# A two-block transformer kernel: modulation rows, attention values and latent key products placed in column groups of the array

## The chip, the cores and the metric

One core of one Trainium2 chip runs the whole program; the other cores are idle. The metric is the device time of one execution in microseconds (us). Three runs of the kernel before took 3384.53, 3387.52 and 3387.95 us; the median is 3387.52 us.

## What is computed

The input is 512 tokens of width 1024. A first block of two layers (latent attention next to a causal convolution, cross attention over 256 memory tokens, a gated FFN) is followed by a second block of one layer (modulated delta-rule mixer, 16 experts with expert choice). The change touches only what stands in the first half of each layer of the first block:

```python
kv = (rms_norm(c_kv, kv_norm_g) @ w_ukv).reshape(B, S, MLA_HEADS, QK_NOPE_DIM + V_HEAD_DIM)
k_nope, v = kv[..., :QK_NOPE_DIM], kv[..., QK_NOPE_DIM:]      # 8 heads, 64 + 64
...
s = q_nope @ k_nope + q_rope @ k_rope                          # per head, chunk-causal
p = softmax(mask(s * scale));  o = p @ v                       # query blocks of 128
...
def adaln_params(cond, w_mod, b_mod):                          # second block, for c and for c_ctx
    return jnp.split(jax.nn.silu(cond) @ w_mod + b_mod, 6, axis=-1)
```

The modulation rows `silu(cond) @ w_mod` (two condition vectors, 1024 x 6144 weights) belong to the second block but are computed during the attention of the first one, half of them in each layer.

## The kernel before

All operands of the products named here are f32. Each engine has its own instruction list, and semaphores (`Signal`, with `at(layer, n)` the n-th event of this layer) order them. PSUM has eight banks `ps[0..7]` of 128 partitions x 512 columns. An engine's list is worked through strictly in order, so an instruction that waits holds back all that stands behind it. The two layers of the first block are one `Fori` loop; what is said of one holds for both.

**Latent products** (PE, from L850 on). With 8 heads: for each head a query product into `ps[h]` (96 rows out, two contraction tiles), then for each head a key product into `ps[h][0:64]` (64 columns of weights, two contraction tiles `k`), then for each of four token tiles a value product into `ps[t]`. ACT copies each result out (L1478, L1481, L1484). Then PE multiplies every query head by a swap matrix (L878), DVE multiplies by the sine (L2049), POOL multiplies by the cosine and adds (L1828, L1831): the rotary embedding. Only when all eight heads are rotated does ACT begin with the exponentials.

**Attention loop.** Step n = 4 x head + query tile, n = 0 to 31. On DVE, each step is: `maximum(n)` (mask L2059, row maximum L2061, scaling L2063), `reciprocal(n-1)` (L2069, which waits for the exponential of step n-1), `tap(n)` (four of the 31 x 4 multiply-adds of the convolution, L2076/L2080), and, at steps 11, 15, 19, ..., `head_out(n//4 - 2)` (L2086), which copies the finished head out of `ps[4][0:64]` and raises `pv_ev`. The last two heads are copied after step 31. On ACT, `exps(h)` is four exponentials (L1496) with the normalisation of older steps between them (L1506); then follow the copy of a modulation row out of PSUM (L1527) and `turned_probs(h-1)`, four copies of transposed probabilities (L1514); then `exps(h+1)`. The order on ACT thus is: exps(h+1), modulation row h, turned probabilities of head h, exps(h+2). On PE the loop is

```python
scores(0); scores(1)
for h in range(HEADS):
    if h < MOD_CHUNKS: modulation_rows(h)      # MOD_CHUNKS = 6
    if h + 2 < HEADS:  scores(h + 2)
    values(h)
    if h < MOD_CHUNKS: modulation_turn(h)
```

`modulation_rows(i)` is eight products (L922) of 2 weight columns by 512 columns into `ps[4][64:66]`; from i = 1 on it waits for `mod_row_ev`, ACT's copy of the row before. `scores` (L893) waits for exponentials to free its banks. `values(h)` transposes the probabilities (L904), four sets of 4, 3, 2, 1 blocks, waits for `pv_ev` of the head before, and multiplies by the values (L911): four products of 512, 384, 256 and 128 columns into `ps[4][0:64]`. `modulation_turn` (L931) turns a row of 512 into four columns with 2 x 128 weights.

After the loop PE computes the keys and values of the cross attention (L766), and then the residual products.

**Traces.** One f32 product shows as two MATMUL and two LDWEIGHTS (PEld) records, so the eight products of `modulation_rows` are sixteen records, the four of `values` are eight.

Of the kernel before, what the change touches and what calls it, by code (L numbers as in the profile page):

```python
# [24 lines left out]
ACT = mybir.ActivationFunctionType  # L25
# [3 lines left out]
P = 128  # L29
D = 1024  # L30
KT = D // P
S = 512
# [63 lines left out]

K_ID, K_ONE, K_SWAP = 0, P, 2 * P
K_FREQ = 3 * P
N_FIRST = K_FREQ + 1
K_TRI, K_STRICT = N_FIRST, N_FIRST + 2 * P  # L100
K_SAME = K_STRICT + 2 * P
K_HALF = K_SAME + P
# [6 lines left out]
def shape_constants():  # L109
    c = np.zeros((P, NCONST), np.float32)  # L110
    i = np.arange(P)
    same = (i[:, None] // CHUNK) == (i[None, :] // CHUNK)
    c[:, K_ID:K_ID + P] = np.eye(P)
    c[:, K_ONE:K_ONE + P] = 1.0
    h = ROPE // 2
    for j in range(h):
        c[NOPE + h + j, K_SWAP + NOPE + j] = -1.0
        c[NOPE + j, K_SWAP + NOPE + h + j] = 1.0
    before = i[:, None] <= i[None, :]
    for d, m in enumerate((before, before.T)):  # L120
        c[:, K_TRI + d * P:K_TRI + (d + 1) * P] = m & same
        c[:, K_STRICT + d * P:K_STRICT + (d + 1) * P] = m & same & (i[:, None] != i[None, :])
    c[:, K_SAME:K_SAME + P] = same

    for u in range(2 * DH):
        for n in range(2):
            c[:, K_HALF + 2 * u + n] = (i // CHUNK) == (n if u < DH else 1 - n)
    c[:, K_IOTA:K_IOTA + CAP] = np.arange(CAP) + 1
    freq = np.float32(10000.0) ** (-np.arange(0, ROPE, 2, dtype=np.float32) / np.float32(ROPE))
    c[:, K_FREQ] = freq[i % h]  # L130
    for g, w in enumerate(WINDOWS):
        def span(n):
            p = np.arange(n)
            return np.clip(p - w // 2 + w, 0, n) - np.clip(p - w // 2, 0, n)
        cnt = (span(ROWS)[:, None] * span(GRID_W)[None, :]).astype(np.float32)
        c[:, K_CNT + g * S:K_CNT + (g + 1) * S] = (np.float32(1.0) / cnt).reshape(1, S)
    return c
# [12 lines left out]
def build(nc, A, out, debug=None):  # L150
    with ExitStack() as ctx:
# [6 lines left out]
        def signal(name, per):  # L158
            return Signal(sem(name), per)
# [53 lines left out]
        ident = consts[:, K_ID:K_ID + P]  # L213
        ones = consts[:, K_ONE:K_ONE + P]
        swap = consts[0:QK, K_SWAP:K_SWAP + QK]

        cqkv = view(0, 4, S)
        qh = view(4 * S, HEADS, S)
# [52 lines left out]
        krot_mm = signal("krot_mm", 1)  # L271
        krot = signal("krot_parts", 2)
        kcopy = signal("kr_in_heads", 1)
        up_mm = signal("up_mm", 20)
        q_ev = signal("q_ev", 8)
        kv_ev = signal("kv_ev", 12)
        qrot_mm = signal("qrot_mm", 8)
# [153 lines left out]
        pos = gates[:, 1, 0:ST * NE].rearrange("p (t e) -> p t e", e=NE)  # L431
        out_tok = view(EXPERTS, 2, D)

        def pair(i):

            return banks[:, 2 * i:2 * i + 2, :].rearrange("p b (h n) -> p (b h) n", n=P)
# [88 lines left out]

        MOD_TILES = 6 * KT // DEPTH

        mod_row = ps[4][VD:VD + 2, :]
# [196 lines left out]
        def _(pe):  # L725
# [21 lines left out]
            with pe.Fori(0, DEPTH) as l:  # L747
# [101 lines left out]

                arrived(C_UP)  # L850
                wuq = w(C_UP, 0, 2, HEADS * QK)
                wukv = w(C_UP, 2 * HEADS * QK, 2, HEADS * (NOPE + VD))
                wv = w(C_UP, 2 * HEADS * QK, 2, HEADS, NOPE + VD)
                pe.wait_ge(glu.sem, glu.at(l, CT))
                pe.wait_ge(lnorm.sem, lnorm.at(l, 2))
                for h in range(HEADS):
# [3 lines left out]
                        pe.wait_ge(lnorm.sem, lnorm.at(l, 4))  # L860
                    mm = product(ps[h], lambda k: wuq[:, k, h * QK:(h + 1) * QK], lambda k: cqkv[:, k, :], 2, m=QK)
                    mm.then_inc(up_mm.sem, 1)
                for h in range(HEADS):
                    pe.wait_ge(q_ev.sem, q_ev.at(l, h + 1))
                    lo = h * (NOPE + VD)
                    mm = product(ps[h], lambda k: wukv[:, k, lo:lo + NOPE], lambda k: cqkv[:, 2 + k, :], 2, m=NOPE)
                    mm.then_inc(up_mm.sem, 1)
                for t in range(ST):
                    pe.wait_ge(kv_ev.sem, kv_ev.at(l, t + 1))
                    mm = product(ps[t], lambda k: cqkv[:, 2 + k, t * P:(t + 1) * P], lambda k: wv[:, k, :, NOPE:], 2)  # L870
                    mm.then_inc(up_mm.sem, 1)
                give_back(1)
                for h in range(HEADS):
                    b = 4 + h % 4
                    pe.wait_ge(kv_ev.sem, kv_ev.at(l, 5 + h % 4))
                    if h >= 4:
                        pe.wait_ge(qrot_sin.sem, qrot_sin.at(l, h - 3))
                    pe.matmul(ps[b][0:QK, :], swap, qh[0:QK, h, :], start=True, stop=True).then_inc(qrot_mm.sem, 1)  # L878
# [17 lines left out]
                def values(h):  # L896
                    for kt in range(ST):
                        n = h * ST + kt
                        if n >= 2:
                            pe.wait_ge(pt_ev.sem, pt_ev.at(l, n - 1))  # L900
                        for t in range(kt, ST):
                            if kt == 0:
                                pe.wait_ge(sc_norm.sem, sc_norm.at(l, h * ST + t + 1))
                            mm = pe.transpose(ps[2 + n % 2][:, t * P:(t + 1) * P],  # L904
                                              probs[:, h % 2, t, kt * P:(kt + 1) * P], ident)
                        mm.then_inc(pt_mm.sem, 1)
                    if h >= 1:
                        pe.wait_ge(pv_ev.sem, pv_ev.at(l, h))
                    for kt in range(ST):
                        pe.wait_ge(pt_ev.sem, pt_ev.at(l, h * ST + kt + 1))  # L910
                        mm = pe.matmul(ps[4][0:VD, kt * P:S], vt[:, kt, h * VD:(h + 1) * VD],  # L911
                                       probsT[:, kt, kt * P:S], start=(kt == 0), stop=(kt == ST - 1))
                    mm.then_inc(pv_mm.sem, 1)


                def modulation_rows(i):
                    arrived(C_MOD + i)
                    wm = w(C_MOD + i, 0, KT, 512)
                    if i >= 1:
                        pe.wait_ge(mod_row_ev.sem, mod_row_ev.at(l, i))  # L920
                    for k in range(KT):
                        mm = pe.matmul(mod_row, cond[:, k, :], wm[:, k, :], start=(k == 0), stop=(k == KT - 1))  # L922
                        if k == 0:
                            say_spent(mm)
                    mm.then_inc(mod_rows.sem, 1)
                    give_back(1)

                def modulation_turn(i):
                    pe.wait_ge(mod_row_ev.sem, mod_row_ev.at(l, i + 1))
                    for j in range(4):  # L930
                        mm = pe.matmul(mod_sum[:, 4 * i + j, :], gates[0:2, i % 2, j * P:(j + 1) * P], ident[0:2, 0:2],  # L931
                                       start=True, stop=True)
                    mm.then_inc(mod_mm.sem, 1)

# [1 line left out]
                scores(0)  # L936
                scores(1)
                for h in range(HEADS):
                    if h < MOD_CHUNKS:
                        modulation_rows(h)  # L940
                    if h + 2 < HEADS:
                        scores(h + 2)
                    values(h)
                    if h < MOD_CHUNKS:
                        modulation_turn(h)
# [462 lines left out]
        def _(act):  # L1408
# [21 lines left out]
            with act.Fori(0, DEPTH) as l:  # L1430
# [46 lines left out]
                    act.wait_ge(up_mm.sem, up_mm.at(l, h + 1))  # L1477
                    nc.scalar.activation(qh[0:QK, h, :], ps[h][0:QK, :], ACT.Copy).then_inc(q_ev.sem, 1)  # L1478
                for h in range(HEADS):
                    act.wait_ge(up_mm.sem, up_mm.at(l, HEADS + h + 1))  # L1480
                    nc.scalar.activation(kh[0:NOPE, h, :], ps[h][0:NOPE, :], ACT.Copy).then_inc(kv_ev.sem, 1)  # L1481
                for t in range(ST):
                    act.wait_ge(up_mm.sem, up_mm.at(l, 2 * HEADS + t + 1))
                    nc.scalar.activation(vt[:, t, :], ps[t][:, :], ACT.Copy).then_inc(kv_ev.sem, 1)  # L1484


# [32 lines left out]
                for h in range(HEADS + 1):  # L1519
                    if h < HEADS:  # L1520
                        exps(h)
                    else:
                        normalise(HEADS * ST - 2)
                        normalise(HEADS * ST - 1)
                    if 1 <= h <= MOD_CHUNKS:
                        act.wait_ge(mod_rows.sem, mod_rows.at(l, h))
                        A1(gates[0:2, (h - 1) % 2, :], mod_row, ACT.Copy).then_inc(mod_row_ev.sem, 1)  # L1527
                    if h >= 1:
                        turned_probs(h - 1)

# [411 lines left out]
        def _(dve):  # L1942
# [29 lines left out]
            with dve.Fori(0, DEPTH) as l:  # L1972
# [109 lines left out]

                def head_out(h):
                    dve.wait_ge(pv_mm.sem, pv_mm.at(l, h + 1))
                    lo = (h % 2) * VD
                    V.tensor_copy(mixT[lo:lo + VD, h // 2, :], ps[4][0:VD, :]).then_inc(pv_ev.sem, 1)  # L2086

                LAG = 1
                for n in range(HEADS * ST + LAG):
# [384 lines left out]
```

## Time and profile before

| | us |
|---|---|
| median of three runs | 3387.52 |
| profiled execution, device time | 3385.13 |
| its span, first to last instruction | 3382.6 |
| PE busy / DVE busy / ACT busy / POOL busy | 2896.7 / 1170.3 / 751.2 / 241.1 |
| mean granted TensorE clock (share of full speed) | 0.939 |
| first layer: latent products to the start of attention | 136 to 191 |
| first layer: attention loop up to the first cross attention product | 191 to 318 |
| second layer: the same two stretches | 1114 to 1170, 1170 to 1295 |

The profile's page gives totals; whether an engine's time counts is read from the chain of work that ended last and from the list of instructions in order of time. A duration is that of one record; the pace of pipelined records is the distance of their starts, which can be shorter. "Granted clock" is 1.00 at 2.4 GHz and 0.50 at 1.2 GHz.

### The profile page before, as it was taken

The numbers are of one execution on the slowest core, as the hardware profiler recorded it, in microseconds if no ns is written. First come the engines' busy times: TensorE is split into PE (matmuls) and PEld (weight loads), VectorE is DVE, ScalarE is ACT, GpSimd is POOL, SyncE is SP. The second block draws the span as 40 slices with busy tenths as digits, with TensorE's granted clock in tenths as the row PEclk, the third lists the DMA queues.
The fourth block names the chain that finished last, engine by engine and source line by source line (L and its number), as shares of the span: only waits on it lengthen the run. The fifth ranks groups of instructions, "written<-read, shape, count | busy, mean of one in ns | idle before, by whom it ended". The sixth has DMA issues, their size and how long they took to land.

```text
span 3382.6 us, 31088 instructions
## 1 busy us (share of the span) xinstructions
PE 2896.7 (86%) x11890; PEld 1825.1 (54%) x11890; DVE 1170.3 (35%) x1663; ACT 751.2 (22%) x1169; POOL 241.1 (7%) x156
## 2 busy tenths in 40 slices
PE   7978888899989798788999959978888758777778
PEld 3324566688854235565888834648788444222223
DVE  0176234433330392544333334364444340000001
ACT  2133232322221242332212131141111022000001
POOL 0120000000000300000000006012332010000000
PEclk9989999999999899999999989889989869999999
DMA  4123211224230132211333231000000026999990
GB/s 143 50 75 120 80 50 57 68 81 113 84 113 22 50 136 88 75 50 50 87 94 100 81 109 44 32 25 1 1 1 1 0 87 275 410 409 410 409 381 25
DMA packets 256104, 379.57 MB, mean 112 GB/s; under 512 B 9153, under 2 KB 170078, under 8 KB 255838
## 3 DMA queue, kind: packets, MB, share of 16 engines
q1 hardware_dynamic: 255966, 377.72, 31.3%
q8 instruction: 88, 1.44, 0.2%
q14 instruction: 50, 0.41, 0.0%
HBM read 375.59 MB, written 2.10 MB: 112 GB/s over the span
## 4 chain that ended last, share of the span: by engine, by line
PE 66%; DMA 13%; DVE 12%; ACT 4%; issue 3%; POOL 1%; SPq 0%; DVEq 0%; ACTq 0%; POOLq 0%; PEldq 0%
PE banks L790 29%; PE banks L766 11%; PE banks L1093 9%; DMA ring<-in_w_up 8%; PE banks L1210 7%; DMA arena<-in_w_down 4%; DVE arena L2080 4%; PE banks L1362 2%; PE banks L776 1%; PE banks L782 1%; PE banks L1025 1%; PE banks L1340 1%; DVE stat L2061 1%; PE banks L1111 1%; DVE arena L2261 1%
## 5 line engine op out<-in xcount | busy, mean ns | idle before, releaser
L1549 ACT ACTIVATE w_hi<-ring 128x2048 fp32r<-128x2048 f32 (+1 forms) x100 | 174.4, 1746 | 544.2 <-PE banks L790 544.2
L790 PE MATMUL banks<-ffn_x_hi,w_hi 128*128 128x512 f32 x704 | 277.7, 394 | 16.7 <-DVE ffn_x_lo L1999 16.6
L790 PE MATMUL banks<-ffn_x_lo,w_hi 128*128 128x512 f32 x704 | 275.6, 391 | 0.0
L790 PE MATMUL banks<-ffn_x_hi,w_lo 128*128 128x512 f32 x704 | 275.4, 391 | 0.0
L1985 DVE TENSOR_TENSOR w_lo<-ring,w_hi 128x2048 fp32r<-128x2048 f32 (+1 forms) x100 | 207.5, 2077 | 78.8 <-ACT w_hi L1549 77.4
L1362 PE MATMUL banks<-ring,std 128*64 128x512 f32 x640 | 153.6, 603 | 46.3 <-DMA ring<-in_w_up 26.5
L766 PE MATMUL banks<-xT,ring 128*128 128x512 f32 (+1 forms) x416 | 183.5, 604 | 1.2 <-ACT taps L1453 1.2
L2080 DVE SCALAR_TENSOR_TENSOR arena<-arena,taps 128x512 f32<-128x512 f32 x240 | 163.3, 743 | 0.0
L790 PEld LDWEIGHTS banks<-ffn_x_hi,w_hi 128*128 128x128 f32 x704 | 132.9, 189 | 51.5 <-issue 17.9
L2449 DVE TENSOR_TENSOR gates<-gates,banks 128x512 f32<-128x512 f32 x16 | 11.0, 688 | 423.9 <-PE banks L1362 423.9
L1093 PE MATMUL banks<-zT,ring 128*128 128x512 f32 x320 | 144.7, 610 | 7.7 <-issue 6.9
L790 PEld LDWEIGHTS banks<-ffn_x_hi,w_lo 128*128 128x128 f32 x704 | 133.2, 189 | 28.0
L790 PEld LDWEIGHTS banks<-ffn_x_lo,w_hi 128*128 128x128 f32 x704 | 133.3, 189 | 26.6
L1210 PE MATMUL banks<-zT,arena 128*128 128x128 f32 x1152 | 141.9, 281 | 5.2 <-DVE zT L2340 4.7
L1210 PEld LDWEIGHTS banks<-zT,arena 128*128 128x128 f32 x1152 | 136.4, 197 | 6.9 <-DVE zT L2340 5.8
L790 PE MATMUL banks<-ffn_hidden_hi,w_hi 128*128 128x512 f32 x352 | 136.9, 389 | 0.0
L790 PE MATMUL banks<-ffn_hidden_lo,w_hi 128*128 128x512 f32 x352 | 136.9, 389 | 0.0
L790 PE MATMUL banks<-ffn_hidden_hi,w_lo 128*128 128x512 f32 x352 | 136.9, 389 | 0.0
L766 PEld LDWEIGHTS banks<-xT,ring 128*128 128x128 f32 (+1 forms) x416 | 79.7, 192 | 104.1 <-issue 104.1
L2182 DVE TENSOR_TENSOR squares<-gates,banks 128x512 f32<-128x512 f32 x44 | 30.2, 687 | 293.6 <-PE banks L790 293.6
L1362 PEld LDWEIGHTS banks<-ring,std 128*64 128x64 f32 x640 | 40.1, 136 | 158.7 <-DMA ring<-in_w_up 64.4
L766 PE MATMUL banks<-arena,ring 128*128 128x256 f32 (+2 forms) x384 | 115.7, 463 | 9.6 <-DVE arena L2036 9.6
(363 smaller groups left out, 4493.6 us busy)
## 6 DMA issues: line engine op xcount, KB each, us to landing
ring<-in_w_up SPq DMA_DIRECT2D x48, 1024.0 KB, 18.4
arena<-in_w_down SPq DMA_DIRECT2D x48, 1024.0 KB, 18.4
ring<-in_ffn_w_in SPq DMA_DIRECT2D x88, 512.0 KB, 4.5
ring<-in_w_gate SPq DMA_DIRECT2D x32, 1024.0 KB, 18.0
ring<-in_w_mod SPq DMA_DIRECT2D x24, 1024.0 KB, 7.2
ring<-in_xa_w_kv SPq DMA_DIRECT2D x16, 1024.0 KB, 6.2
zT<-in_w_gate SPq DMA_DIRECT2D x16, 1024.0 KB, 18.5
zT<-in_w_up SPq DMA_DIRECT2D x16, 1024.0 KB, 18.4
```

The lines of the kernel that those rows point to most:

```text
L766: mm = pe.matmul(bank[0:m, 0:width], weights(k), rhs(k), start=(k == 0), stop=(k == n - 1))
L776: mm = pe.matmul(ps[bank][:, :], ones, zT[:, t, :], start=(t == 0), stop=(t == KT - 1))
L782: mm = pe.matmul(ps[bank + 1][:, :], ones, squares[:, t % 2, :], start=(t == 0), stop=(t == KT - 1))
L790: mm = pe.matmul(bank[:, :], weights(wp, k), rhs(rp, k), start=(k == 0 and wp == rp), stop=(k == n - 1 and wp == 1))
L1025: mm = pe.matmul(ps[4 + v][:, :], xv[:, kt, h * XD + v * P:h * XD + (v + 1) * P], probsT[:, kt, :], start=(kt == 0), stop=(kt == MT - 1))
L1093: mm = pe.matmul(out, weights(k), rhs(k), start=(k == 0), stop=(k == n - 1))
L1111: mm = pe.matmul(ps[1 + m % 2][:, 0:n], ones, squares[:, t % 2, 0:n], start=(t == 0), stop=(t == KT - 1))
L1210: pe.matmul(o, lhsT(un), rhs(un), start=True, stop=True)
L1362: mm = pe.matmul(bank[n * CAP:(n + 1) * CAP, :], tokens, weights[:, n * 512:(n + 1) * 512], start=first, stop=last)
L1549: nc.scalar.activation(w_split[n % 2][0][:, 0:m], raw[n % 2][:, 0:m], ACT.Copy).then_inc(f_hi.sem, 1)
L1985: V.tensor_tensor(lo[:, 0:m], raw[n % 2][:, 0:m], hi[:, 0:m].bitcast(F32), ALU.subtract).then_inc(f_lo.sem, 1)
L2080: V.scalar_tensor_tensor(out=acc, in0=x, scalar=c, in1=acc, op0=ALU.mult, op1=ALU.add)\
```

## The change

Three groups of products are written to different column groups of the array, that is, to different partition ranges of one PSUM bank: the keys of two heads to partitions 0-63 and 64-127; the values of a head as query blocks 0 and 3 to 0-63 and blocks 1 and 2 to 64-127; the eight modulation products to partitions 0-1, 32-33, 64-65 and 96-97 in turn, added up by `modulation_turn`, whose moving operand becomes a 98 x 2 selection matrix. Because the modulation rows now lie where `values` writes, `modulation_rows(i)` waits for `pv_ev` (DVE's copy of head i-1) in place of `mod_row_ev`, `values(h)` waits for `mod_row_ev`, and the loop issues `scores(h + 2)` ahead of `modulation_rows(h)`. `head_out` copies in two instructions. Two constant columns are added.

```diff
-                for h in range(HEADS):
+                for h in range(0, HEADS, 2):
                     pe.wait_ge(q_ev.sem, q_ev.at(l, h + 1))
-                    lo = h * (NOPE + VD)
-                    mm = product(ps[h], lambda k: wukv[:, k, lo:lo + NOPE], lambda k: cqkv[:, 2 + k, :], 2, m=NOPE)
+                    for k in range(2):
+                        for j in range(2):
+                            mm = pe.matmul(ps[h][j * NOPE:(j + 1) * NOPE, :], wkv[:, k, h + j, 0:NOPE], cqkv[:, 2 + k, :],
+                                           start=(k == 0), stop=(k == 1))
                     mm.then_inc(up_mm.sem, 1)
                 for t in range(ST):
-                    pe.wait_ge(kv_ev.sem, kv_ev.at(l, t + 1))
+                    pe.wait_ge(kv_ev.sem, kv_ev.at(l, t // 2 * 2 + 2))
...
                 for h in range(HEADS):
                     b = 4 + h % 4
-                    pe.wait_ge(kv_ev.sem, kv_ev.at(l, 5 + h % 4))
+                    if h in (0, 2):
+                        pe.wait_ge(kv_ev.sem, kv_ev.at(l, 6 + h))
...
                     if h >= 1:
                         pe.wait_ge(pv_ev.sem, pv_ev.at(l, h))
+                    if h < MOD_CHUNKS:
+                        pe.wait_ge(mod_row_ev.sem, mod_row_ev.at(l, h + 1))
                     for kt in range(ST):
                         pe.wait_ge(pt_ev.sem, pt_ev.at(l, h * ST + kt + 1))
-                        mm = pe.matmul(ps[4][0:VD, kt * P:S], vt[:, kt, h * VD:(h + 1) * VD],
-                                       probsT[:, kt, kt * P:S], start=(kt == 0), stop=(kt == ST - 1))
+                        v = vt[:, kt, h * VD:(h + 1) * VD]
+                        if kt == 0:
+                            pe.matmul(outer(ps[4][0:VD, :]), v, outer(probsT[:, 0, :]), start=True, stop=False)
+                        else:
+                            mm = pe.matmul(ps[4][0:VD, 3 * P:S], v, probsT[:, kt, 3 * P:S], start=False, stop=(kt == 3))
+                        if kt < 3:
+                            q0 = max(kt, 1) * P
+                            pe.matmul(ps[4][VD:2 * VD, q0:3 * P], v, probsT[:, kt, q0:3 * P], start=(kt == 0), stop=(kt == 2))
...
                     if i >= 1:
-                        pe.wait_ge(mod_row_ev.sem, mod_row_ev.at(l, i))
+                        pe.wait_ge(pv_ev.sem, pv_ev.at(l, i))
                     for k in range(KT):
-                        mm = pe.matmul(mod_row, cond[:, k, :], wm[:, k, :], start=(k == 0), stop=(k == KT - 1))
+                        mm = pe.matmul(mod_part[k % 4], cond[:, k, :], wm[:, k, :], start=(k < 4), stop=(k >= 4))
...
-                        mm = pe.matmul(mod_sum[:, 4 * i + j, :], gates[0:2, i % 2, j * P:(j + 1) * P], ident[0:2, 0:2],
+                        mm = pe.matmul(mod_sum[:, 4 * i + j, :], gates[0:MOD_ROWS, i % 2, j * P:(j + 1) * P], add_rows,
                                        start=True, stop=True)
...
                 for h in range(HEADS):
+                    if h + 2 < HEADS:
+                        scores(h + 2)
                     if h < MOD_CHUNKS:
                         modulation_rows(h)
-                    if h + 2 < HEADS:
-                        scores(h + 2)
                     values(h)
...
-                        A1(gates[0:2, (h - 1) % 2, :], mod_row, ACT.Copy).then_inc(mod_row_ev.sem, 1)
+                        A1(gates[0:MOD_ROWS, (h - 1) % 2, :], ps[4][0:MOD_ROWS, :], ACT.Copy).then_inc(mod_row_ev.sem, 1)
...
-                    lo = (h % 2) * VD
-                    V.tensor_copy(mixT[lo:lo + VD, h // 2, :], ps[4][0:VD, :]).then_inc(pv_ev.sem, 1)
+                    dst = mixT[(h % 2) * VD:(h % 2 + 1) * VD, h // 2, :]
+                    V.tensor_copy(outer(dst), outer(ps[4][0:VD, :]))
+                    V.tensor_copy(dst[:, P:3 * P], ps[4][VD:2 * VD, P:3 * P]).then_inc(pv_ev.sem, 1)
```

`outer(x)` is the view of `x` that holds its first and its last 128 columns.

## Rows read from the trace of the kernel before

**Rows 1.** Chain of work that ended last, first layer: start us, us, what.

```profile
136.12 36.58 PE banks L766 x80
...
178.77 1.26 POOL arena L1828
...
243.74 2.07 DVE arena L2080 x3
...
317.78 55.30 PE banks L766 x192
```

**Rows 2.** Busy by stretch: us, PE, PEld, DVE, ACT, POOL, clock, DMA.

```profile
255.00:270.00 15.00, 14.48 (x52) 5.62 (x50) 14.70 (x35) 6.52 (x18) 0.00 (x0) 1.00 0.40 141
195.00:210.00 15.00, 8.14 (x12) 2.06 (x13) 14.29 (x35) 4.82 (x14) 0.00 (x0) 0.59 0.03 2
```

**Rows 3.** Instructions in order of time, key products: start us, us, engine, line.

```profile
152.17 0.14 PEld L766 LDWEIGHTS banks<-arena,ring 128*64 128x64 f32 x1 [0.29 <-issue]
...
155.38 0.59 ACT L1481 ACTIVATE arena<-banks 64x512 f32<-64x512 f32 x1 [1.13 <-PE banks L766]
...
164.62 0.14 PEld L766 LDWEIGHTS banks<-arena,ring 128*64 128x64 f32 x1 [0.29 <-issue]
...
165.57 7.13 PE L766 MATMUL banks<-ring,arena 128*128 128x512 f32 x16
```

**Rows 4.** Instructions in order of time, expert products, and PE by stretch.

```profile
2840.62 7.07 PE L1362 MATMUL banks<-ring,std 128*64 128x512 f32 x32
...
2817.60:2817.65 0.05, 0.05 (x2) 1.00 0.00 0
...
2818.05:2818.10 0.05, 0.05 (x4) 1.00 0.00 0
```

**Rows 5.** Instructions in order of time, one turn of the attention loop.

```profile
253.98 7.03 PE L922 MATMUL banks<-ring,cond 128*2 128x512 f32 x16
...
260.85 0.69 DVE L2061 TENSOR_REDUCE stat<-banks 128x1 f32<-128x512 f32 x1
...
262.96 0.59 ACT L1527 ACTIVATE gates<-banks 2x512 f32<-2x512 f32 x1
263.56 0.93 PE L904 MATMUL banks<-consts,zT 128*128 128x128 f32 x7
264.27 1.68 ACT L1514 ACTIVATE arena<-banks 128x512 f32<-128x512 f32 x4 [0.72 <-PE banks L904]
264.35 0.68 DVE L2086 COPY arena<-banks 64x512 f32<-64x512 f32 x1
...
265.04 0.11 DVE L2059 MEMSET banks<- 64x64 f32 x1
...
265.84 0.37 ACT L1496 ACTIVATE zT<-banks,stat 128x128 f32<-128x128 f32 x1
...
268.52 0.42 DVE L2061 TENSOR_REDUCE stat<-banks 128x1 f32<-128x256 f32 x1
...
269.05 0.15 DVE L2069 RECIPROCAL stat<-stat 128x1 f32<-128x1 f32 x1
```

**Rows 6.** Instructions in order of time, start of the loop; PE by stretch at a lull.

```profile
206.66 9.28 PE L922 MATMUL banks<-ring,cond 128*2 128x512 f32 x16
...
217.97 0.69 ACT L1496 ACTIVATE zT<-banks,stat 128x512 f32<-128x512 f32 x1 [2.78 <-DVE stat L2063]
...
224.66 0.15 DVE L2069 RECIPROCAL stat<-stat 128x1 f32<-128x1 f32 x1
...
300.00:301.00 1.00, 0.98 (x4) 0.50 0.00 0
```

**Rows 7.** Instructions in order of time, last two heads of each layer.

```profile
308.68 4.53 PE L911 MATMUL banks<-arena 128*64 128x512 f32 x8
...
315.42 2.37 PE L911 MATMUL banks<-arena 128*64 128x512 f32 x8
...
1287.37 3.58 PE L911 MATMUL banks<-arena 128*64 128x512 f32 x8
```

More of the change, by code:

```diff
@@ L98 @@
 K_FREQ = 3 * P
-N_FIRST = K_FREQ + 1
+K_SEL = K_FREQ + 1
+N_FIRST = K_SEL + 2
 K_TRI, K_STRICT = N_FIRST, N_FIRST + 2 * P
@@ L130, in shape_constants @@
     c[:, K_FREQ] = freq[i % h]
+    for n in range(2):
+        c[:, K_SEL + n] = i % 32 == n
     for g, w in enumerate(WINDOWS):
@@ L215, in build @@
         swap = consts[0:QK, K_SWAP:K_SWAP + QK]
+        MOD_ROWS = 3 * 32 + 2
+        add_rows = consts[0:MOD_ROWS, K_SEL:K_SEL + 2]
         cqkv = view(0, 4, S)
@@ L273, in build @@
         kcopy = signal("kr_in_heads", 1)
-        up_mm = signal("up_mm", 20)
+        up_mm = signal("up_mm", HEADS + HEADS // 2 + ST)
         q_ev = signal("q_ev", 8)
@@ L432, in build, with outer @@
         out_tok = view(EXPERTS, 2, D)
+        def outer(x):
+            return x.rearrange("p (t n) -> p t n", n=P)[:, 0:ST:ST - 1, :]
         def pair(i):
@@ L526, in build @@
         MOD_TILES = 6 * KT // DEPTH
-        mod_row = ps[4][VD:VD + 2, :]
+        mod_part = [ps[4][32 * g:32 * g + 2, :] for g in range(4)]
         mod_sum = ps[5][:, 0:2 * MOD_TILES].rearrange("p (j w) -> p j w", w=2)
@@ L851, in _ @@
                 wuq = w(C_UP, 0, 2, HEADS * QK)
-                wukv = w(C_UP, 2 * HEADS * QK, 2, HEADS * (NOPE + VD))
-                wv = w(C_UP, 2 * HEADS * QK, 2, HEADS, NOPE + VD)
+                wkv = w(C_UP, 2 * HEADS * QK, 2, HEADS, NOPE + VD)
                 pe.wait_ge(glu.sem, glu.at(l, CT))
@@ L862, in _ @@
                     mm.then_inc(up_mm.sem, 1)
-                for h in range(HEADS):
+                for h in range(0, HEADS, 2):
                     pe.wait_ge(q_ev.sem, q_ev.at(l, h + 1))
-                    lo = h * (NOPE + VD)
-                    mm = product(ps[h], lambda k: wukv[:, k, lo:lo + NOPE], lambda k: cqkv[:, 2 + k, :], 2, m=NOPE)
+                    for k in range(2):
+                        for j in range(2):
+                            mm = pe.matmul(ps[h][j * NOPE:(j + 1) * NOPE, :], wkv[:, k, h + j, 0:NOPE], cqkv[:, 2 + k, :],
+                                           start=(k == 0), stop=(k == 1))
                     mm.then_inc(up_mm.sem, 1)
                 for t in range(ST):
-                    pe.wait_ge(kv_ev.sem, kv_ev.at(l, t + 1))
-                    mm = product(ps[t], lambda k: cqkv[:, 2 + k, t * P:(t + 1) * P], lambda k: wv[:, k, :, NOPE:], 2)
+                    pe.wait_ge(kv_ev.sem, kv_ev.at(l, t // 2 * 2 + 2))
+                    mm = product(ps[t], lambda k: cqkv[:, 2 + k, t * P:(t + 1) * P], lambda k: wkv[:, k, :, NOPE:], 2)
                     mm.then_inc(up_mm.sem, 1)
@@ L1479, in _ @@
                 for h in range(HEADS):
-                    act.wait_ge(up_mm.sem, up_mm.at(l, HEADS + h + 1))
-                    nc.scalar.activation(kh[0:NOPE, h, :], ps[h][0:NOPE, :], ACT.Copy).then_inc(kv_ev.sem, 1)
+                    act.wait_ge(up_mm.sem, up_mm.at(l, HEADS + h // 2 + 1))
+                    src = ps[h // 2 * 2][h % 2 * NOPE:(h % 2 + 1) * NOPE, :]
+                    nc.scalar.activation(kh[0:NOPE, h, :], src, ACT.Copy).then_inc(kv_ev.sem, 1)
                 for t in range(ST):
-                    act.wait_ge(up_mm.sem, up_mm.at(l, 2 * HEADS + t + 1))
+                    act.wait_ge(up_mm.sem, up_mm.at(l, HEADS + HEADS // 2 + t + 1))
                     nc.scalar.activation(vt[:, t, :], ps[t][:, :], ACT.Copy).then_inc(kv_ev.sem, 1)
```

## The prediction

> **What bounds the kernel now.** I read the chain of work that ended last first, since the three groups of products lie in two short stretches of each layer and totals say nothing of them. The reader is to see three owners in turn [rows 1]: PE through the latent products (36.58 us from 136.12), then the POOL and DVE rotary work, then DVE alone through the attention loop (its convolution taps, three or four to a step), and PE again from the first cross attention product at 317.78. Next, the busy time by stretch: in the loop DVE is busy 14.70 of 15 us, ACT 6.52; PE shows 14.48 at full clock, but is nowhere on the chain there [rows 2]. So a faster PE is worth its whole gain ahead of the rotary work, nothing inside the loop, and something again behind the last head. The list in order of time then gives the prices, and the order of waits in the code tells what the change does to DVE's cover.
>
> **1. Key products, a gain.** Weight loads of the keys start at 152.17 and, 29 records later, at 164.62: 0.43 us a record, so 32 records (16 products) are 13.7 us [rows 3]. What does putting two in different column groups bring? The expert products already do that with 64 columns each: 32 records in 7.07 us, less 0.2 of drain, is 0.215 us a record, half of the above, and at their start two records begin in the same 0.05 us [rows 4]. So the keys take 6.9 us instead of 13.7: 6.9 us a layer. Next in line could be ACT: a key copy is 0.59 us [rows 3], two to a pair of heads make 1.2 us against 1.7 us of PE, so PE stays the slower. The rotary work, the scores and DVE's loop all hang on the last query rotation and move forward whole. Two layers: **-13.8 us**.
>
> **2. head_out in two copies, a loss.** No copy of 256 columns from PSUM is in the trace. DVE's reduction costs 0.69 us for 512 columns and 0.42 for 256 [rows 5]; two of the small kind are 0.15 above one large, less some overlap. I take 0.13 (bounds 0 and 0.3). Six of the eight in a layer lie in DVE's loop: 12 x 0.13 = **+1.6 us**.
>
> **3. The new order on PE, a loss.** This is the large term. Before, modulation row h was computed early: sixteen records in 7.03 us in the shadow of DVE's steps, 253.98 to 261.0 [rows 5]. Now it waits for `pv_ev` h, which DVE raises when its copy of head h-1 ends, and that copy is the last thing in step 4h+7, just ahead of the mask instruction of step 4h+8 (265.04 in the turn shown, copy from 264.35) [rows 5]. Behind it wait, on PE, the transposes of head h; on ACT, the copy of the row, then the four copies of turned probabilities, and behind these the exponential of step 4h+8. DVE needs that exponential for the reciprocal in step 4h+9, at 269.05, that is 4.0 us after 265.04 [rows 5]; its taps stand behind that wait and cannot fill it.
> How long is the new path? (a) The wake-up is 0.1 us. (b) The row: eight products in four groups are two rounds. A product is two records of 0.43 us at full clock, so a round is 0.86, two are 1.7, and with 0.2 of drain 1.9 us; at half clock 3.4 + 0.2 = 3.6. (c) From the end of the row to the exponential's end: the row's copy 0.59 with its start-up 0.65, the transposes beside it (the first copy of turned probabilities starts 0.71 after the first transpose, 263.56 to 264.27, so hidden), from there to the exponential's start 1.57 (264.27 to 265.84), its 0.37, and 0.07 to DVE: 2.7 us [rows 5].
> Which clock? In the new turn PE works densely for some 6 us, and then, since all scores but the first two of a head wait for DVE's slow steps, has two products in the next 8 us. That is the picture of 195 to 210, where the mean granted clock is 0.59 [rows 2], and at 300, between two sets of transposes, it stood at 0.50 [rows 6]. Once at half speed, PE got back late: the row at 206.66 took 9.28 us against 7.03, so ran at half speed for 2 x 2.25 = 4.5 us [rows 5, 6]; the values at 308.68 took 4.53 against 2.37, the ones at 1287.37 3.58 [rows 7], 4.3 and 2.4 us at half speed. So I take half clock for the row and part of the transposes (+0.35). The reciprocal is ready at 0.1 + 3.6 + 2.7 + 0.35 = 6.7 us, due at 4.0: a stall of 2.7 us, five times a layer (h = 1 to 5). For h = 0 there is no `pv_ev` wait, but the row now follows the last of scores(2), which waits for the exponential that ends at 218.66: 218.8 + 1.7 (scores at half clock) + 3.6 + 2.7 = 226.8 against 224.66 [rows 6], some 2.4 us with the slower transposes. A layer loses 5 x 2.7 + 2.4 = 15.9: **+31.8 us** for two. Bounds: at full clock 0.7 a head, none at h = 0, 7 us in all; with the row and the transposes wholly at half clock 3.4 and 3, 40 us.
>
> **4. Values in two groups.** Per group 640 columns instead of 1280, in order of issue 640 columns' time, 1.1 + 0.2 us at full clock against 2.37 [rows 7]. Inside the loop DVE does not wait for it. Behind step 31 PE, with ACT, is alone on the path: the values of heads 6 and 7 both count. In the first layer the 4.53 becomes about 2.4 (half clock) with somewhat more of head 7's transposes at half clock, and the 2.37 becomes 1.2: 2.6 us; in the second 1.1 + 1.1, about 2.1. I take 4.5 for both together: **-4.5 us** (bounds 2 and 6).
>
> **5. Nothing for the rest.** The turn of the modulation row keeps its columns; 98 weight rows instead of 2 do not lengthen a load whose 128 columns stay. The weights of the rows are given back about a third of a turn later, yet each chunk has two turns to land. Cover gone there would show as PE waiting for `w_mod`.
>
> **Sum.** -13.8 + 1.6 + 31.8 - 4.5 = +15.1 us on the profiled execution's 3385.1 (span 3382.6 and 2.5 around it) is 3400.2. The median is 2.4 us above that execution, so the forecast is 3402.
>
> **The skill against the rows.** Rows show two groups at exactly twice the pace, four groups are in no row. The Trainium skill ("TensorE: Matmul & The Clock Gate", Measured speedup vs the span model) gives 2.38 times for three column groups and 3.07 for four row groups; as an estimate from that page, the row at half clock would take 13.7 / 3.07 = 4.5 us, the stall 0.9 more in each of twelve turns, and the sum +26. Its page "TensorEngine Tiling (Array Packing)", Performance Considerations, speaks for column groups wherever weights have at most 64 columns; that looks at PE alone, and by it only the gains of terms 1 and 4 would be left, 3371.
>
> **Rivals.**
> A. *PE keeps or regains full clock* before the row (the row of layer two began at half speed too, but the clock's return came at different distances, 2.4 to 4.5 us above). Then term 3 is +7 at the least: -13.8 + 1.6 + 7 - 4.5 = -10, 3377 to 3378. For it: faster windows exist, and the loop was at 1.00 before. Against it: the long lull. Chance 0.14.
> B. *The stall is half as large* (clock back within about 2 us of the row's start): 1.5 a turn, 18 in all, sum +1, 3389. This is no change that can be measured: on this kernel about 0.2%, 7 us, is what a measurement can tell. Chance 0.14.
> C. *Four groups run no faster than two* (or pair by pair). The row takes four rounds, 7 us at half clock, or 5.5 where the clock returns midway; the stall is 4.6 to 6, times twelve 55 to 72: sum +38 to +55, 3426 to 3442. For it: only two groups are in the rows. Chance 0.10.
> D. *The wait never binds*, since DVE would find something I misread to do: the gains alone, 3371. Against it: the lists are in order, and reciprocal stands before the taps. Chance 0.05. The other side of the forecast is A: it decides at a stall of 1.4 us a turn, (13.8 + 4.5 - 1.6) / 12, which is a row of 2.6 us where nothing is slow behind it.
> The change might also not do side by side what it says (the keys in particular); the expert rows make that unlikely, 0.02, and it would add 14 to 50.
> Forecast: 0.55, with its own range 3392 to 3413.
>
> **Chances.** Slower by over 0.2% (above 3394): most of the forecast's 0.55, C, the last, 0.67 together. Within 0.2%: B and the forecast's low edge, 0.16. Faster: A, D, 0.17. The range leaves out D and the far half of C: 3374 to 3425.
>
> **What would show it.** Keys: weight loads in pairs, 6.9 us, rotary work 6.9 earlier. Row: eight products at four to a start, 1.9 or 3.6 us long, starting right behind the second copy of head_out. DVE idle before L2069 for ACT's L1496, twelve times, 2 to 3 us each; the clock near 0.5 where the rows start. Tail: 2 us shorter. Wrong it is if DVE's idle time before L2069 is under 1 us (A) or over 4 (C).

## The result, and the profile after

The changed kernel takes 3398.57 us (median of seven executions, 3396.53 to 3399.45) against 3387.51 us: a ratio of 1.0035, with a 95% interval of 1.0023 to 1.0047. It is 11.1 us slower. The profiled execution has a span of 3396.6 us, 14.0 more than before, and a mean granted clock of 0.919 instead of 0.939. Forecast were 3402 us and a range of 3374 to 3425.

All lines of the changed kernel have moved: the key products are now L875, the modulation row L941, the transposes L915, the values L926 to L931, head_out L2106 and L2107, the reciprocal L2089, the exponential L1516.

**The keys.** Instructions of the changed kernel in order of time, columns as in [rows 3]: the 32 records of the key products, ACT's copies, the value products.

```profile
150.13 7.09 PE L875 MATMUL banks<-arena,ring 128*64 128x512 f32 x32
...
150.61 0.14 PEld L875 LDWEIGHTS banks<-arena,ring 128*64 128x64 f32 x2 [0.28 <-issue]
...
152.11 1.21 ACT L1501 ACTIVATE arena<-banks 64x512 f32<-64x512 f32 x2 [1.28 <-PE banks L875]
...
157.14 7.13 PE L775 MATMUL banks<-ring,arena 128*128 128x512 f32 x16
```

Weight loads come two at a time every 0.43 us, and the stretch is 7.09 us, against some 13.9 before [rows 3]. ACT is idle 0.5 us or more before each pair of copies, so PE still sets the pace.

**The turn of the loop.** Instructions of the changed kernel in order of time, to be read beside [rows 5].

```profile
228.87 0.41 DVE L2106 COPY arena<-banks 64x256 f32<-64x256 f32 x1
229.29 0.43 DVE L2107 COPY arena<-banks 64x256 f32<-64x256 f32 x1
229.73 0.11 DVE L2079 MEMSET banks<- 64x64 f32 x1
229.86 3.58 PE L941 MATMUL banks<-ring,cond 128*2 128x512 f32 x16 [0.68 <-DVE arena L2107]
...
233.37 0.98 PE L915 MATMUL banks<-consts,zT 128*128 128x128 f32 x7
233.52 0.60 ACT L1547 ACTIVATE gates<-banks 98x512 f32<-98x512 f32 x1 [6.06 <-PE banks L941]
...
234.14 1.68 ACT L1534 ACTIVATE arena<-banks 128x512 f32<-128x512 f32 x4
...
235.71 0.37 ACT L1516 ACTIVATE zT<-banks,stat 128x128 f32<-128x128 f32 x1
...
236.20 0.16 DVE L2089 RECIPROCAL stat<-stat 128x1 f32<-128x1 f32 x1 [2.38 <-ACT zT L1516]
```

The reader follows one line of cause: the second copy ends at 229.72, the row starts, ACT copies it, then the turned probabilities, then comes the exponential, and DVE has stood for 2.38 us. The chain of work of the changed kernel shows the same as its owner changes from DVE to PE and ACT and back (start us, us, what):

```profile
1213.49 0.44 DVE arena L2107
...
1214.07 3.59 PE banks L941 x16
1217.66 1.06 PE banks L915 x4
1218.82 0.61 ACT arena L1534
```

The waits of DVE in the first layer's half (who waited for whom: us in total, times, longest), the kernel before first, then the changed one:

```profile
DVE stat L2069 <- ACT zT L1496: 0.4, 1, 0.4
```

```profile
DVE stat L2089 <- ACT zT L1516: 14.4, 7, 3.0
DVE arena L2106 <- PE banks L928: 6.3, 2, 3.9
DVE arena L2100 <- issue: 0.3, 1, 0.3
```

The second layer has 14.3 us in 7 waits. One of the seven is the old 0.4, so six new waits stand in each layer, 28.0 us in both layers together. Their mean is 2.3 us; the single ones go from 1.5 to 3.0. The line of L2106 is DVE waiting for the values products of the last two heads behind step 31: 6.3 us, where the kernel before has 10.0. PE by stretch in the changed kernel (us, busy, clock, DMA), the two stretches of [rows 2]:

```profile
195.00:210.00 15.00, 5.74 (x8) 0.50 0.00 0
255.00:270.00 15.00, 9.47 (x37) 0.66 0.25 81
```

The clock was 0.59 and 1.00 there before. The loop of the changed kernel stands 8.5 us earlier in time, so the two stretches do not hold the same work; over the whole loop of the first layer, from the mask of step 0 to the turned probabilities of head 6, the mean granted clock is 0.67, against 0.90 before.

**The books.** Each layer is closed by itself, from marks that do not depend on when the program's first transfers landed. From the mask of step 0 to the turned probabilities of head 6, the first layer takes 132.45 us (182.33 to 314.78) instead of 116.38 (190.83 to 307.21): +16.1. From there to the first cross attention product it takes 7.1 us instead of 10.5. The key stretch gives 6.9. That is +5.8 in the first layer; in the second, taken from the last query copy on, the same marks give -6.9, +16.0 and -1.8, that is +7.3. Of the 13 us of both, the medians show 11.1 and the two profiled spans 14.0; a single execution wanders by more than the difference.

### The profile page after: what moved, and what is told of

The parts are those of the page before. It is cut to its first block, busy times and chain, and to the rows that moved or that the text cites. A ratio compares the mean times of both kernels' runs of the same rounds, so it can differ in the third digit from the quotient of the medians.

```text
span 3396.6 us, 31276 instructions
## 1 busy us (share of the span) xinstructions
PE 2849.0 (84%) x11986; PEld 1813.7 (53%) x11986; DVE 1175.0 (35%) x1679; ACT 749.6 (22%) x1169; POOL 241.2 (7%) x156
## 3 DMA queue, kind: packets, MB, share of 16 engines
q8 instruction: 89, 1.46, 0.2%
## 4 chain that ended last, share of the span: by engine, by line
PE 67%; DMA 13%; DVE 11%; ACT 5%; issue 3%; POOL 1%; SPq 0%; DVEq 0%; ACTq 0%; POOLq 0%; PEldq 0%
PE banks L799 29%; PE banks L775 10%; PE banks L1112 9%; DMA ring<-in_w_up 8%; PE banks L1229 7%; DMA arena<-in_w_down 4%; DVE arena L2100 3%; PE banks L1381 2%; PE banks L785 1%; PE banks L941 1%; PE banks L791 1%; PE banks L1044 1%; PE banks L1359 1%; PE banks L1130 1%; DVE arena L2282 1%
## 5 line engine op out<-in xcount | busy, mean ns | idle before, releaser
L2100 DVE SCALAR_TENSOR_TENSOR arena<-arena,taps 128x512 f32<-128x512 f32 x240 | 163.5, 744 | 0.6 <-issue 0.6
L904 PE MATMUL banks<-arena 96*128 96x128 f32 (+3 forms) x128 | 76.2, 715 | 95.1 <-ACT zT L1516 76.8
```

Source lines behind the costliest of these rows:

```text
L904: pe.matmul(ps[sc_bank[t]][:, 0:(t + 1) * P], qh[0:QK, h, t * P:(t + 1) * P], kh[0:QK, h, 0:(t + 1) * P], start=True, stop=True).then_inc( ...
L2100: V.scalar_tensor_tensor(out=acc, in0=x, scalar=c, in1=acc, op0=ALU.mult, op1=ALU.add)\
```

## The experiments

Times are medians; the kernel before is given as it ran beside each group: 3385.58 with the keys, the order and wait, the fillers of the loop, and the early head_out with the rows first; 3385.18 with the two groups, the one group, the values in one group, and the early head_out with the scores first; 3386.42 with the last three. Differences are taken to it, since its median moves by 2 us from group to group.

**The keys alone.** The edit of the change in the latent products, on the kernel before:

```diff
-                for h in range(HEADS):
+                for h in range(0, HEADS, 2):
...
+                            mm = pe.matmul(ps[h][j * NOPE:(j + 1) * NOPE, :], wv[:, k, h + j, 0:NOPE], cqkv[:, 2 + k, :],
+                                           start=(k == 0), stop=(k == 1))
```

> The kernel before with the key products alone paired in two column groups. Theory: the key stretch takes 7 us instead of 13.8 in each layer, the rotary work and the attention loop move forward whole, so 3373.7 us, 13.8 below the kernel before. Rival (something behind it, ACT's copies or a transfer, ends at its old time anyway): within 3 us of the kernel before.

Measured: 3371.36 us, 14.2 below the kernel before, ratio 0.9956 (0.9942 to 0.9969). Nothing behind the key products takes the gain back.

**Order and wait alone.** The kernel before, with

```diff
-                        pe.wait_ge(mod_row_ev.sem, mod_row_ev.at(l, i))
+                        pe.wait_ge(pv_ev.sem, pv_ev.at(l, i))
...
+                    if h + 2 < HEADS:
+                        scores(h + 2)
                     if h < MOD_CHUNKS:
                         modulation_rows(h)
-                    if h + 2 < HEADS:
-                        scores(h + 2)
```

> The kernel before with the loop's new order and the new wait alone: modulation row h behind scores(h+2) and waiting for DVE's copy of head h-1; all products stay in one group. Theory (the row and what ACT does behind it lie on DVE's path): a row of 16 records in series from half clock takes about 9.3 us, so a stall of 0.1 + 9.3 + 2.7 - 4.0 = 8.1 us in ten turns and about 8 in the two first ones, some 97 us: 3484 us (3465 to 3500). Rival (the wait is covered by the taps): 3388 us.

Measured: 3481.08 us, 95.5 above the kernel before, ratio 1.0282 (1.0268 to 1.0296). The waits of DVE in its first layer:

```profile
DVE stat L2069 <- ACT zT L1496: 48.6, 7, 8.6
```

Eight microseconds a turn (7.1 to 8.7), as computed. So the two edits that only make room in the bank bring the whole loss of the loop, and the row in four groups is what brings it down to 28 us; what the groups are worth is measured by themselves below. The two edits were not parted here.

**Filler products, to hold the clock.** The changed kernel, with

```diff
+                        if 2 <= h and t >= 1:
+                            for _ in range((0, 3, 3, 1)[t]):
+                                pe.matmul(ps[5][:, 64:S], ident, cosT[:, 64:S], start=True, stop=True)
```

> The changed kernel with filler products of 448 columns by PE into unread columns of bank 5 (three each behind the second and third score product of heads 2 to 7, one behind the fourth), so that the clock stays at full speed until the row starts. Theory (half of the row's time is the half clock): the row takes 1.9 us instead of 3.6, a stall of 0.7 instead of 2.4 in ten turns, none in the first two, so 20 us less than the changed kernel: 3378 us. Rival (the stall is the wait chain itself, whatever the clock): 3398 us.

Measured: 3377.93 us, 7.7 below the kernel before and so 19 below the changed kernel, ratio to before 0.9977 (0.9968 to 0.9986). A row in order of time, then PE by stretch (us, busy, clock, DMA), then DVE's waits in the first layer:

```profile
243.70 1.90 PE L944 MATMUL banks<-ring,cond 128*2 128x512 f32 x16 [1.00 <-DVE arena L2110]
```

```profile
240.00:247.00 7.00, 4.89 (x29) 1.00 0.12 23
```

```profile
DVE stat L2092 <- ACT zT L1519: 4.3, 7, 0.7
```

The same stretch of the changed kernel:

```profile
240.00:247.00 7.00, 3.72 (x4) 0.51 0.00 1
```

The two stretches are the same in time, not in work: the row of this turn starts at 243.70 here and at 247.41 in the changed kernel. Taken up to the start of the row alone, the clock is 1.00 from 236.00 to 243.70 with the fillers and 0.50 from 240.41 to 247.41 without them. More work on PE made the kernel faster: the row takes 1.90 us instead of 3.4 in the mean, the wait 0.70 in ten turns (0.45 and 0.63 in the first turn of each layer) instead of 2.3. This is rival A, brought about by the fillers.

**Two groups, and one.** The changed kernel with fewer groups for the row (the selection matrix of `modulation_turn` is changed to fit):

```diff
-                        mm = pe.matmul(mod_part[k % 4], cond[:, k, :], wm[:, k, :], start=(k < 4), stop=(k >= 4))
+                        mm = pe.matmul(mod_part[k % 2], cond[:, k, :], wm[:, k, :], start=(k < 2), stop=(k >= 6))
```

> The changed kernel with the eight modulation products in two column groups instead of four. Theory (the stall is the row's length, and groups give their full factor): four rounds instead of two, the first 3.6 us at half clock, so a row of 5.5 us instead of 3.6 and a stall of 4.3 instead of 2.4 us in twelve turns, 23 us more than the changed kernel: 3421 us. Rival (four groups ran no faster than two would): 3398 us.

Measured: 3430.63 us, 45.4 above the kernel before, ratio 1.0130 (1.0114 to 1.0145), which is 34 above the changed kernel where 23 was expected. With `mod_part[0]` for all eight:

> The changed kernel with the eight modulation products in one column group, one after the other. Theory: eight rounds, a row of 8.9 us and a stall of 7.7 us in twelve turns, 64 us more than the changed kernel: 3462 us. Rival (the stall is set by something else than the row): less than 20 us more.

Measured: 3469.93 us, 84.8 above the kernel before, ratio 1.0250 (1.0235 to 1.0266), 74 above the changed kernel. One row in each, third head of the first layer, two groups first, then one:

```profile
252.93 6.34 PE L941 MATMUL banks<-ring,cond 128*2 128x512 f32 x16 [0.81 <-DVE arena L2107]
```

```profile
257.80 9.71 PE L941 MATMUL banks<-ring,cond 128*2 128x512 f32 x16 [0.81 <-DVE arena L2107]
```

Both expectations were too low for the same reason: the rows took 6.2 to 6.5 and 9.5 to 9.9 us where I had 5.5 and 8.9. At full clock the sixteen records take 7.03 us in one group [rows 5] and half of that, 3.6 with the drain, in two. 9.71 and 6.34 are each 2.7 us above, so PE ran at half clock for 5.4 us and not for the 3.6 I had put in; the granted clock says the same, 0.50 from 257.80 to 263.20 in the run with one group. Only the first row of each layer was shorter (5.66 us, and 8.91 and 9.07). The direction and the cause stand: the stall is the row's length, and four groups are not the same as two.

**Values in one group, head_out in one copy.** The changed kernel with that part undone:

```diff
-                            pe.matmul(outer(ps[4][0:VD, :]), v, outer(probsT[:, 0, :]), start=True, stop=False)
...
+                        mm = pe.matmul(ps[4][0:VD, kt * P:S], vt[:, kt, h * VD:(h + 1) * VD],
+                                       probsT[:, kt, kt * P:S], start=(kt == 0), stop=(kt == ST - 1))
...
+                    V.tensor_copy(dst, ps[4][0:VD, :]).then_inc(pv_ev.sem, 1)
```

> The changed kernel with the values products in one group and head_out in one copy again. Theory: 5 us lost behind the last head in both layers together, 2 us won on DVE by the single copy, nothing else, since DVE does not wait for the values inside the loop: 3 us more than the changed kernel, 3401.5 us. Rival (the values in two groups shorten the turn as well): 12 us more or above.

Measured: 3398.92 us, 13.7 above the kernel before, ratio 1.0041 (1.0027 to 1.0055); the changed kernel has 11.1, and the intervals overlap, so the 3 us are neither shown nor excluded. The rival of 12 us is out. The trace shows a term I had not listed. In order of time:

```profile
246.63 3.17 PE L935 MATMUL banks<-ring,cond 128*2 128x512 f32 x16 [0.63 <-DVE arena L2100]
```

In the first layer its rows take 3.1 to 3.3 us from the second head on, those of the changed kernel 3.2 to 3.6, and DVE's waits are 12.0 us instead of 14.4. In the second layer the rows take 3.4 to 3.6 and the waits are 14.3 us in both kernels. That longer values products leave more of the clock is shown (mean granted clock 0.926 to 0.928 in all five executions, against 0.919 to 0.921 in the seven of the changed kernel). That this shortens DVE's waits is seen in one layer of one execution and not in the other, so a price of the shorter values inside the loop is not shown. Behind the loop their gain is plain: from the turned probabilities of head 6 to the first cross attention product the two layers take 10.0 and 10.1 us here, 7.1 and 7.5 in the changed kernel.

**head_out early, scores still first.** The changed kernel, with

```diff
-                    if n >= 2 * ST and n % ST == 3:
+                    if n >= 2 * ST and n % ST == 1:
                         head_out(n // ST - 2)
```

> The changed kernel with head_out two steps earlier, but the scores still ahead of the modulation row. Theory (order and wait both hold the row back, since the last score product of a turn waits for the exponential of step 4h+7): the row starts right behind that product, only 0.6 us earlier in ten turns, 3392 us. Rival (the wait for head_out alone was the cause): 3370 us.

Measured: 3394.22 us, 9.0 above the kernel before, ratio 1.0023 (1.0013 to 1.0034). That is 2 us less than the changed kernel's 11.1, where I expected 6 and the rival 28; the intervals overlap, so even the 2 us are not shown. DVE's waits are 14.3 and 11.9 us in the two layers. The wait for head_out is not the sole cause: with the scores first, the row stands behind the last score product of the turn all the same. In order of time:

```profile
229.53 2.08 PE L904 MATMUL banks<-arena 96*128 96x512 f32 x2 [2.20 <-ACT zT L1516]
231.38 0.11 DVE L2079 MEMSET banks<- 64x64 f32 x1
...
231.53 3.59 PE L941 MATMUL banks<-ring,cond 128*2 128x512 f32 x16
...
237.89 0.16 DVE L2089 RECIPROCAL stat<-stat 128x1 f32<-128x1 f32 x1 [2.41 <-ACT zT L1516]
```

The row starts as the score product, at half clock, is through, and that is 0.15 us behind the mask of step 4h+8; in the changed kernel it was 0.13. My 0.6 us was wrong because the copy, moved out of this step, no longer lengthens it: the mask comes 0.86 us earlier too, and the wait stays 2.4 us.

**head_out early, rows first again.** Both edits together:

```diff
                 for h in range(HEADS):
-                    if h + 2 < HEADS:
-                        scores(h + 2)
                     if h < MOD_CHUNKS:
                         modulation_rows(h)
+                    if h + 2 < HEADS:
+                        scores(h + 2)
...
-                    if n >= 2 * ST and n % ST == 3:
+                    if n >= 2 * ST and n % ST == 1:
```

> The changed kernel with head_out two steps earlier (after steps 4h+1 instead of 4h+3) and modulation_rows ahead of scores(h+2) again. Theory (the loss is only the late start of the row): the row runs beside steps 4h+6 and 4h+7, DVE waits nowhere, 28 us less than the changed kernel, 17 below the kernel before: 3370 us. Rival (DVE now waits for the values products of the head before, or the scores come late): 3385 to 3398 us.

Measured: 3369.45 us, 16.1 below the kernel before, ratio 0.9952 (0.9939 to 0.9966). In order of time, and DVE's waits in the first layer:

```profile
249.37 0.43 DVE L2107 COPY arena<-banks 64x256 f32<-64x256 f32 x1
...
249.94 3.59 PE L941 MATMUL banks<-ring,cond 128*2 128x512 f32 x16 [3.98 <-DVE arena L2107]
```

```profile
DVE stat L2089 <- ACT zT L1516: 1.2, 2, 0.8
```

The row still takes 3.59 us at half clock and still follows a copy, but DVE no longer waits for it: it now has two steps of DVE, 7 us, above it. Of the 1.2 us that are left in the layer, 0.4 is the old wait and 0.8 stands behind step 31. This kernel has every product of the change in its groups and keeps the gain. The clock in its loop is lower than before all the same, 0.74 against 0.90. The rows first with the copy left where it was did not run, so what the order costs alone, without the late copy, stays open; the copy alone, in the run above, gives no gain that is shown.

**The tail alone, and with fillers.** The kernel with the keys paired, its loop as before, and only heads 6 and 7 in two groups (`if h < MOD_CHUNKS:` the old product and copy, else the new ones):

> The kernel before with the paired keys, and with the values of heads 6 and 7 alone in two groups (and their copies in two instructions); rows, order and waits of the loop as before. Theory (the values gain only behind the last step, and only these two heads lie there): the 13.8 us of the keys and 5 us of the two tails, nothing lost in the loop: 3367 us, 18 to 19 below the kernel before. Rival (the tail's gain is lost to the clock or to the cross attention products behind it): 3371 us, as with the keys alone.

Measured: 3365.99 us, 20.4 below the kernel before, ratio 0.9942 (0.9928 to 0.9955). This is the lowest median of the versions without fillers, the groups where PE is on the path and the old products where it is not; but its interval overlaps those of the early head_out and of the keys alone, so the order of the three is not shown by the times. The traces show the tail: from the turned probabilities of head 6 to the first cross attention product it takes 7.6 and 7.8 us in the two layers, with the keys alone 10.4 and 10.5. Then with

```diff
+                        if h == 6 and kt == 1:
+                            for _ in range(5):
+                                pe.matmul(ps[5][:, 64:S], ident, cosT[:, 64:S], start=True, stop=True)
```

> As the kernel with the keys paired and heads 6 and 7 in two groups, and with five filler products of 448 columns by PE behind the first two sets of transposes of head 6, where PE is idle for 7 us. Theory (the first values products behind the loop run at half clock only because of that idle time): 1.1 us a layer of the values and 0.3 of the transposes are won, 3364 us. Rival (the fillers outlast the idle time, or the clock falls nevertheless): 3367 us or above.

Measured: 3365.60 us, ratio 0.9940 (0.9926 to 0.9953), no better that the times could show. In order of time, first layer:

```profile
292.66 3.92 PE L915 MATMUL banks<-cosT,consts 128*128 128x448 f32 x10
299.99 0.90 PE L910 MATMUL banks<-consts,zT 128*128 128x128 f32 x3 [3.41 <-ACT arena L1534]
300.82 0.69 PE L926 MATMUL banks<-arena 128*64 128x256 f32 x1
```

The fillers ran at full clock and so were over after 3.92 us, not the 6 I had sized them for; PE idled 3.41 us after them and was at half clock again (0.69 for a product that takes 0.43 at full clock). So for the first layer the idea has not been tried in a form that could work. In the second layer it did work:

```profile
1262.35 5.15 PE L915 MATMUL banks<-cosT,consts 128*128 128x448 f32 x10
1269.27 0.71 PE L910 MATMUL banks<-consts,zT 128*128 128x128 f32 x3 [1.77 <-ACT arena L1534]
1269.91 0.43 PE L926 MATMUL banks<-arena 128*64 128x256 f32 x1
```

There the fillers began at half clock and took 5.15 us, PE idled 1.77 us behind them, and the first values product ran at full clock (0.43). The tail of that layer is 5.8 us against 7.8 without fillers, 2.0 won in the trace; one such gain is within what a median moves.

**Two copies alone.** The kernel before, with head_out as `tensor_copy` of columns 0 to 255 and of 256 to 511:

> The kernel before with head_out in two copies of 256 columns each, nothing else. Theory: 0.17 us more in each of twelve turns, 2 us: within the measurement of the kernel before, its profiled span up by 1 to 3 us. Rival (the second copy costs a full start-up, 0.4 us): 5 us more.

Measured: 3385.95 us, 0.5 below the kernel before, ratio 1.0000 (0.9991 to 1.0009). In order of time:

```profile
263.19 0.41 DVE L2086 COPY arena<-banks 64x256 f32<-64x256 f32 x1
263.53 0.41 DVE L2087 COPY arena<-banks 64x256 f32<-64x256 f32 x1
263.95 0.11 DVE L2059 MEMSET banks<- 64x64 f32 x1
```

Start to next instruction is 0.76 us, against 0.69 for the single copy [rows 5], so 0.07 a turn where I expected 0.17, and the rival's 5 us is out; in the changed kernel, where the first copy takes two blocks apart from each other and the second reads other partitions, it is 0.86. Which of the two makes the difference is not shown.

## Why the prediction was right

- **Bound and cover.** Right. The chain gave PE ahead of the rotary work, DVE in the loop; the keys alone gave 14.2 us where 13.8 had been put in.
- **The stall (term 3).** Right in its mechanism and nearly in size: 2.3 us a turn in the mean against 2.7 and 2.4, 28 us for both layers instead of 31.8. The sum 0.1 + row + 2.7 - 4.0, with the row as it was in each turn, meets nine of the twelve waits within 0.1 us; the other three (2.98, 2.96, 2.85) are 0.5 to 0.6 longer, and there the transposes were slow (1.49 us for seven, or 2.67 for all ten in one run). Two things were put in too high: the rows took 3.4 us in the mean, not 3.6 (one took 2.7), and the 0.35 for slower transposes was 0.15 in the mean, for in most turns the clock was back when they began (0.98 for seven, against 0.93 before). The order and wait alone, the fillers, and the early head_out with the rows first each moved the time by what the sum says, within 3 us; the early head_out alone did not (2 us instead of 6), and the runs with two groups and one lost 11 and 10 us more than expected, through the half clock that lasted longer.
- **Copies (term 2).** 0.17 a copy instead of 0.13. Five copies of a layer, not six, stand between two steps of DVE (the sixth comes behind step 31), so the term is 1.7 us against 1.6: the two slips nearly cancel.
- **Tail (term 4).** 3.4 and 1.8 us against 2.6 and 2.1: 5.2 instead of 4.5. In the first layer the clock came back sooner after the restart than before. Part of this is chance: in the other traces with the old products this tail takes 10.0 to 10.5 us, so the 9.3 of the second layer before was a short one.
- **Missing.** Some 2.4 us. The step with the wait is longer than before by the wait and 0.13 us more (in the first turn 6.08 us instead of 3.47, with a wait of 2.48), 1.6 us in twelve turns: a reciprocal that need not wait starts 0.08 before the instruction ahead of it ends, and its taps follow 0.07 behind it, not 0.10 (236.20 to 236.30). And in one turn of each layer the taps start 0.3 us late (`DVE arena L2100 <- issue`), for which no run shows a cause. The smaller stall (3.8 us) and the larger gain of the tail (0.7) outweigh it: +15.1 was forecast, and the two layers closed by themselves give +13.1. So the number is nearly right in part because terms missed in opposite directions.
- **The rest (term 5).** Right: the turn of the row takes 1.05 us with 98 weight rows as with 2, and PE waits nowhere for `w_mod`.
- **Rivals.** A was wrong here but true as a mechanism, as the fillers show; it needs PE to be kept busy. B's 1.5 us a turn came once in twelve (1.46), where the clock returned early, and not in the mean. C fell: a row in four groups takes 1.90 us at full clock against 7.03 for one, and with the half clock in them the rows of two groups took 6.2 to 6.5 us where those of four took 3.2 to 3.6. D fell with the twelve waits. In the chances, A and D make 0.19, not 0.17, and the 0.67 counts the whole of the forecast's 0.55, whose low edge is counted again with B; the sides stay the same. The Trainium skill's 3.07 times for four row groups ("TensorE: Matmul & The Clock Gate", Measured speedup vs the span model) would have made it, as an estimate, 4.5 us at half clock; the trace has 3.59, so this stream of f32 products in four column groups gets the full factor. The Trainium skill's page "TensorEngine Tiling (Array Packing)", Performance Considerations, goes by the width of the weights, by which 3371 us would have come; "PE alone" was too strong, since the same section warns of the copies out of PSUM (1.7 us here), but of waits in another engine's list it says nothing. The versions that keep DVE's cover do come out at 3366 to 3369.

## What to carry to other kernels

A bank that two jobs share joins their queues: ask, before giving the second job the first one's partitions, which engine frees them, at what point of its list, and who stands behind the job that now waits. A product that is four times shorter can lose to a longer one that started 11 us earlier (253.98, against a copy that ends at 265.03 [rows 5]). Spread products over column groups where PE is on the path, and leave them where it is hidden: their shortening buys nothing there and lets the clock fall (0.74 against 0.90 in the loop of the early head_out). That costs nothing as long as DVE covers the row, and half of the row's speed where it does not.

## What the runs showed of the hardware that was not expected

Products of f32 with 2 weight columns in four column groups begin four at a time and reach the whole factor: sixteen records in 1.90 us, drain included, against 7.03, that is 3.7 times as they stand and 4.0 without some 0.2 us of drain in each. Seven filler products of 448 columns in a turn kept the granted clock at 1.00 up to the row, where it was 0.50 without them, and the kernel was 19 us faster for it. How long PE stayed at half clock after it began to work again was not the same from turn to turn: rows that take 7.03 us at full clock took 9.5 to 9.9 in the run with one group (8.9 and 9.1 at the start of the loops), and 8.3 to 9.9 in the run with the order and wait alone.
